# A two-layer hybrid backbone step in float32: 24 rows of the prompt tile's expert products moved out of the attention heads, scores taken negated, one inverse root for four gate inputs

## What is computed

```python
h = x * (1.0 + scale1) + shift1
q, k, v, su, sv = project_heads(h, w_in)        # su, sv through gelu
attn = latent_attention(q, k, v, ctx_k, ctx_v, sink)   # 8 heads; softmax over [sink, scores]
sg = u * (einsum('gpq,bnqgc->bnpgc', w_s, layer_norm(v)) + b_s)   # u = su, v = sv
y = concatenate([attn, sg]) @ w_o
x = layer_norm(ALPHA * x + gate1 * y)
h = x * (1.0 + scale2) + shift2
...
q = (x @ w_q).reshape(n, 8, 2, 128)             # peer(h, ...)
s1, s2 = q[:, :, 0] @ key1.T, q[:, :, 1] @ key2.T
idx, g = top 16 of the sums of the two top 16   # per token and head: 128 experts of 16384
a = einsum('thkd,td->thk', u_tab[idx], h)       # "u rows": dot products
out = einsum('thk,thkd->td', gelu(a) * g, v_tab[idx])  # "v rows": weighted sum
x = layer_norm(ALPHA * x + gate2 * out)
```

## Time and profile before

| | |
|---|---|
| median of 3 runs | 3826.93 us (3823.88 to 3830.95) |
| the profiled execution, its own time | 3821.99 us |
| its span, first to last instruction | 3820.2 us |
| PE busy | 3482.8 us (91%) |
| VectorE busy | 2808.7 us (74%) |
| ScalarE busy | 855.0 us (22%) |
| GpSimd busy | 1600.8 us (42%) |
| HBM traffic | 330 GB/s over the span |
| mean granted clock of PE | 0.946 |

### The profile page before, as it was taken

One profiled execution on the slowest core, in us unless ns is written; L12 is line 12 of the kernel. 1 busy time (PEld: TensorE's weight loads), 2 busy tenths in 40 slices (PEclk: granted clock), 3 DMA queues, 4 the chain that ended last, 5 costly groups with the idle time before them and its releaser, 6 DMA issues.

```text
span 3820.2 us, 38450 instructions
## 1 busy us (share of the span) xinstructions
PE 3482.8 (91%) x12478; PEld 2127.3 (56%) x12478; DVE 2808.7 (74%) x6205; ACT 855.0 (22%) x2198; POOL 1600.8 (42%) x1362
## 2 busy tenths in 40 slices
PE   6897889998889999999988878999988999999996
PEld 2554445888778444444336443478877864444443
DVE  1489769878776875666756897698877768766668
ACT  1104301156642000000021151111765210000000
POOL 2046336213641355555510761542146323555553
PEclk9896889999999999999989878999998999999998
DMA  9877569878999999999984974888899998999995
GB/s 345 326 264 281 187 231 346 315 262 304 409 399 327 352 355 414 413 413 413 386 311 137 368 247 139 295 329 317 282 345 408 377 357 314 388 413 414 413 404 230
DMA packets 413991, 1263.48 MB, mean 331 GB/s; under 512 B 36241, under 2 KB 139665, under 8 KB 370785
## 3 DMA queue, kind: packets, MB, share of 16 engines
q0 software_dynamic: 192000, 721.61, 49.3%
q1 hardware_dynamic: 171808, 514.19, 36.0%
q10 hardware_dynamic: 49984, 25.23, 2.2%
HBM read 1174.06 MB, written 86.84 MB: 330 GB/s over the span
## 4 chain that ended last, share of the span: by engine, by line
PE 48%; DMA 22%; DVE 16%; POOL 7%; issue 6%; ACT 1%; ACTq 0%; SPq 0%; DVEq 0%; POOLq 0%
PE P L919 23%; DMA ring<-in_peer_u_dram,eidx 10%; DMA ring<-in_peer_v_dram,eidx 10%; POOL ring L660 7%; PE P L893 6%; PE T L931 5%; DVE ring L1268 5%; PE P L947 4%; PE P L743 4%; DMA ring<-in_w_mod_dram 2%; PE V L947 1%; PE O L947 1%; DVE h L1286 1%; PE T L726 1%; PE T L905 1%
## 5 line engine op out<-in xcount | busy, mean ns | idle before, releaser
L660 POOL DMA_INDIRECT ring<-in_peer_u_dram,eidx x768 | 939.9, 1224 | 1300.9 <-DVE ring L1268 810.1
L1268 DVE SCALAR_TENSOR_TENSOR ring<-ring,h 128x1024 f32<-128x1024 f32 x768 | 925.0, 1223 | 278.5 <-DMA ring<-in_peer_u_dram,eidx 258.1
L947 PE MATMUL P<-w_ring,area 128*128 128x512 f32 x2048 | 933.9, 599 | 44.4 <-DVE area L1442 44.4
L919 PE MATMUL P<-hT,w_ring 128*128 128x256 f32 x4096 | 925.0, 384 | 0.0
L660 POOL DMA_INDIRECT ring<-in_peer_v_dram,eidx x512 | 621.1, 1213 | 673.9 <-DVE late L1286 401.4
L919 PEld LDWEIGHTS P<-hT,w_ring 128*128 128x128 f32 x4096 | 781.9, 194 | 103.9
L947 PEld LDWEIGHTS P<-w_ring,area 128*128 128x128 f32 x2048 | 390.7, 192 | 549.8 <-issue 549.6
L1286 DVE SCALAR_TENSOR_TENSOR h<-ring,dots,h 128x1024 f32<-128x1024 f32 x254 | 326.0, 1283 | 157.7 <-DMA ring<-in_peer_v_dram,eidx 144.5
L1286 DVE SCALAR_TENSOR_TENSOR late<-ring,dots,late 128x1024 f32<-128x1024 f32 x254 | 325.6, 1282 | 18.2 <-DMA ring<-in_peer_v_dram,eidx 2.8
L893 PE MATMUL P<-hT,w_ring 128*128 128x128 f32 (+1 forms) x1024 | 289.1, 444 | 2.9 <-issue 2.2
L947 PE MATMUL V<-w_ring,qT 128*128 128x512 f32 x512 | 261.4, 592 | 0.0
(11 more groups left out here) (219 smaller groups left out, 3367.2 us busy)
## 6 DMA issues: line engine op xcount, KB each, us to landing
w_ring<-in_peer_uT_dram SPq DMA_DIRECT2D x128, 1024.0 KB
w_ring<-in_peer_vB_dram SPq DMA_DIRECT2D x128, 1024.0 KB
ring<-in_w_mod_dram POOLq DMA_DIRECT2D x48, 1024.0 KB, 8.3
w_ring<-in_peer_wq_dram SPq DMA_DIRECT2D x64, 512.0 KB
h<-acts_d SPq DMA_DIRECT2D x64, 512.0 KB
w_ring<-in_w_in_dram SPq DMA_DIRECT2D x48, 512.0 KB
area<-gate_d SPq DMA_DIRECT2D x16, 1536.0 KB, 14.6
hT<-gate_d SPq DMA_DIRECT2D x16, 1536.0 KB, 12.9
```

The lines of the kernel that those rows point to most:

```text
L660: pool.indirect_dma_start(out=ring[:, b, :], out_offset=None, in_=tables["uv".index(phase)], in_offset=bass.IndirectOffsetOnAxis(ap=eidx[: ...
L919: mm = pe.matmul(out[:, 0:TOKENS], w[:, c * P:(c + 1) * P], hT[:, c, TOKENS:2 * TOKENS], start=c == 0, stop=c == DC - 1)
L947: mm = pe.matmul(bank[ACC[2 * t + half]][:, :], w, uv_ring[:, b // 2 % (WR // 2), b % 2, half * 512:(half + 1) * 512], start=b == 0, stop= ...
L1268: dve.scalar_tensor_tensor(ring[:, b, :], ring[:, b, :], 1.0, h2[:, k, :], ALU.mult, ALU.mult, accum_out=dots[:, k, row:row + 1]).then_inc ...
```

## The change

Five edits, in the order of the program:

1. *Rows.* `prompt_rows` now counts rows. In group S: 16 in the projection and 24 ahead of the attention as before; behind a head 1, in heads 2 and 5 of each tile 2 (40 in all, before 64); 8 behind the last head and the wait for `rows_in`, ahead of the first residual; 40 behind the residuals (before 24). ScalarE's `gelu_dots(0)` stands ahead of query block 4 instead of 2, and VectorE's `expert_weights(0)` and v rows begin at key block 4 instead of 3: the same 64 rows over 12 key blocks instead of 13.
2. *Negated scores.* VectorE scales by -1/8, adds the mask and takes the minimum with the negated sink; what it gets is the negated maximum. The instruction L1530 and its semaphore are gone; ScalarE's exponentials take `scale=-1.0` and wait for the score bank's emptied counter. The sinks are negated once per layer, in group P.
3. *One inverse root.* `sv_stats` takes the statistics of all the group's tiles ahead of the first head and computes their inverse roots together, in columns of the tensor `r1`. `norm_sv` keeps the scaling and the two products.
4. *Positions in the u sweep.* Slot transposes behind blocks 45, 77 and 104 (before 47, 78 and 105). Chunks from block 48 over 28 blocks, from 79 over 23, from 106 over 17 (before 50 over 27, 80 over 22, 107 over 16).
5. ScalarE's `top_softmax` and `gelu_dots(1)` stand one or two blocks earlier.

```diff
-SLOT_BLOCKS = {47: 3, 78: 4, 105: 1}
-CHUNK_BLOCKS = [(3, 50, 27), (4, 80, 22), (1, 107, 16)]
+SLOT_BLOCKS = {45: 3, 77: 4, 104: 1}
+CHUNK_BLOCKS = [(3, 48, 28), (4, 79, 23), (1, 106, 17)]
...
-                            act.wait_ge(probs_max, l * (TILES * HEADS) + (k * HEADS + h + 1))
-                            act.activation(esink[:, h:h + 1], sink[:, h:h + 1], ACT.Exp, bias=negmax[:, k % 2, h:h + 1]
-                                           ).then_inc(sink_exp, 1)
+                            job = ("score", g, t, h)
+                            act.wait_ge(emptied[BANK[job]], emptied_at(job, l))
+
+                            act.activation(esink[:, h:h + 1], sink[:, h:h + 1], ACT.Exp, scale=-1.0,
+                                           bias=negmax[:, k % 2, h:h + 1]).then_inc(sink_exp, 1)
...
-                        if g == "S" and j == 2:
+                        if g == "S" and j == 4:
                             gelu_dots(0)
...
+                def sv_stats(g):
+
+                    nt = len(GROUPS[g])
+                    for t in range(nt):
+                        job = ("in", g, 3, t)
+                        dve.wait_ge(emptied[BANK[job]], emptied_at(job, l))
+                        link(dve.bn_stats(stats[:, 0, :], sv[:, t, :]))
+                        link(dve.bn_aggr(sv_mean[:, t, :], stats[:, 0:1, :]))
+                    var, y, half, other = sv_mean[:, 0:nt, 1], sv_rstd[:, 0:nt], sv_nr[:, 0, 0:nt], sv_nr[:, 1, 0:nt]
+                    note(dve.tensor_scalar(half, var, EPS, -0.5, ALU.add, ALU.mult))
+                    link(dve.tensor_scalar(other, var, EPS, None, ALU.add))
+                    link(dve.tensor_single_scalar(other.bitcast(U32), other.bitcast(U32), 1, ALU.logical_shift_right))
+                    link(dve.tensor_scalar(y.bitcast(U32), other.bitcast(U32), -1.0, float(0x5f3759df), ALU.mult, ALU.add))
+                    for _ in range(3):
+                        link(dve.tensor_tensor(other, y, y, ALU.mult))
+                        link(dve.tensor_tensor(other, other, half, ALU.mult))
+                        link(dve.scalar_tensor_tensor(y, other, 1.5, y, ALU.add, ALU.mult))
+
                 def norm_sv(g, t):
-                    job = ("in", g, 3, t)
-                    dve.wait_ge(emptied[BANK[job]], emptied_at(job, l))
-                    layer_norm_stats(sv[:, t, :], AW)
+                    link(dve.tensor_scalar(sv[:, t, :], sv[:, t, :], sv_mean[:, t, 0:1], sv_rstd[:, t:t + 1],
+                                           ALU.subtract, ALU.mult))
...
+                    if g == "P":
+                        link(dve.tensor_scalar(sink[:], sink[:], -1.0, None, ALU.mult))
+                    sv_stats(g)
...
-                                                           HD ** -0.5, sink[:, h:h + 1], ALU.add, ALU.max,
-                                                           maxs[:, k % 2, h:h + 1]), job)
-                            dve.tensor_scalar(negmax[:, k % 2, h:h + 1], maxs[:, k % 2, h:h + 1], -1.0, None,
-                                              ALU.mult).then_inc(probs_max, 1)
+                                                           -HD ** -0.5, sink[:, h:h + 1], ALU.add, ALU.min,
+                                                           negmax[:, k % 2, h:h + 1]), job)
...
-                                prompt_rows(1)
+                                prompt_rows(2 if h in (2, 5) else 1)
...
                     dve.wait_ge(rows_in, (2 * l + (gi + 1)) * 48)
+                    if latent:
+
+                        prompt_rows(GP)
...
-                        prompt_rows(12)
+                        prompt_rows(SLOTS - 24 - 16 - 40 - GP)
...
-                        if latent and j == 3:
+                        if latent and j == 4:
                             expert_weights(0)
-                        if latent and j >= 3:
-                            add_rows(0, PV_EARLY * (j - 3) // 13, PV_EARLY * (j - 2) // 13)
+                        if latent and j >= 4:
+                            add_rows(0, PV_EARLY * (j - 4) // 12, PV_EARLY * (j - 3) // 12)
```

24 lines of the change are left out of this document (12 added, 12 removed).

## The result

The changed kernel takes 3802.31 us (median of 4 runs, 3794.20 to 3804.24), the kernel before 3828.94 beside it (4 runs, 3823.88 to 3833.62). The ratio is 0.9924, with a 95% interval of 0.9909 to 0.9939: 29 us less by the ratio, where 77 were forecast. The direction was right; 3802 lies outside the range of 3730 to 3786.

The account below looks back on a forecast made before the run. The prediction took VectorE to bound the latent attention, PE the u sweep, and left the v sweep unchanged. Per layer, -31 us in attention and -7.5 in query and u sweep gave 3827 - 77 = 3750 us, range 3730 to 3786.

Parts of the forecast that it names:

- The sum, -38.5 us per layer: Whole kernel: attention -31 and query and u sweep -7.5 us per layer, -77 us for both layers.
- Rows between the heads, -27.2 us per layer: Latent attention: 64 rows between heads become 40, so 24 x 1.135 = 27.2 us leave VectorE per layer.
- PE takes over the attention: Rival: PE's 100 us at clock 0.73 plus 17 us of waits limit the attention's gain to 15.5; 3781 us, chance 0.13.
- Negation and root, -8.1: Latent attention: removing the negation saves VectorE 2.6 us and the shared inverse root 5.5 us per layer.
- 8 rows ahead of the residuals: 0: After the last head: the rows may overrun VectorE's wait, but the last projection tile sets the end; cost 0, at most 3 us.
- 40 rows end at T+62, PE keeps 5.7 us: Behind the last residual tile, done at T: rows end at T+62, ahead of block 4's key products; PE stays 5.7 us earlier.
- VectorE 6 to 7 us later against T: After keys and their 64 rows, taking 109 us as before, VectorE is 6 to 7 us later against the last residual's end.
- PE waits about 5 us at the slots, -7.5 us for query and u sweep: Tile 3's slot transposes, u sweep: PE waits about 5 us for VectorE, yet the transposes come 7.5 us earlier per layer.
- From there on the one-hots set the pace: U sweep behind tile 3's slots: one-hots set the pace, and PE's wait of 8.42 us falls to about 5.
- The burst starves: Rival: the sixteen added gathers behind the residuals run slowly, rows end 12 us later; 3775 us, chance 0.18.
- Slower: Rival: PE's clock stays at 0.50 through the attention, so PE needs 147 us there; 3839 us, chance 0.03.
- Nothing: Rival: what leaves the heads comes back whole in the burst and the sweep; 3827 us, chance 0.02.

Follow-up runs that it names:

- e9: The change with tile 3's exponentials behind block 41, 24 rows between the heads instead of 40 and 56 behind the residuals instead of 40: 3809.3 us, one run.
- e4: The kernel before with only the negation gone from the heads and the one inverse root; rows and places as before: 3803.6 us, ratio 0.9933.
- e8: e1 with the 8 rows ahead of the residuals moved behind them, 48 there: 3807.9 us, ratio 0.9942.
- e1: The change with only tile 3's exponentials moved, from behind u block 33 to behind block 41: 3782.5 us, ratio 0.9875.
- e11: e6 with tile 4's slot transposes behind block 74 instead of 77, chunks of tiles 3 and 4 over 26 blocks each: 3771.3 us.
- e15: The kernel before with the change's moved rows and places alone, without the negation and norm edits: 3817.7 us, ratio 0.9971.
- e6: The change with 48 rows between the heads instead of 40, 32 behind the residuals instead of 40, tile 3's exponentials behind block 39: 3770.9 us, ratio 0.9844.
- e12: e6 with the third head's score products of the latent group repeated seven times in place, in PE's wait ahead of its first share: 3768.2 us.
- e10: e6 with 8 of the 24 rows ahead of the first head moved between the heads (16 ahead, 56 between): 3758.1 us, ratio 0.9808.
- e14: e1 with 32 rows between the heads instead of 40 and 48 behind the residuals instead of 40: 3793.8 us, one run.
- e7: e4 with tile 3's exponentials behind block 38, its slots behind 43, its chunks from block 46 over 30 blocks: 3795.7 us, ratio 0.9910.

## Why the prediction was wrong

- **The sum, -38.5 us per layer.** In the profiled executions the attention gave 20.2 and 20.9 us, and from the projection's first product to the v sweep the layers took 12.4 and 14.2 us more where 7.5 less had been forecast. Together that is 14.5 us less for both layers. The two executions lie 19.8 us apart, of which 3.3 are their starts and 2.6 the way from one layer's v sweep to the next one's first score; the medians lie 27 apart.
- **Rows between the heads, -27.2 us per layer.** Wrong as a term. VectorE's time fell by that, but the stage didn't: by the series above, 24 rows less save 13 to 15 us. I charged 4 us for PE, and VectorE's waits for PE's scores came to 12.5. PE's clock was to rise above 0.8 and was 0.76. The rival "PE takes over the attention" had part of the mechanism: in the change PE is busy 101.7 us of 125 and waits 23.9, where the rival had 100 and 17. But it isn't a floor, as the 114.6 us of e9 show. The rival's numbers also mix two bases: 118 us is a length of the whole stage, 25 less than 143, while its gain of 15.5 is counted from 133 us of heads. The measured gain lies between 15.5 and 31, the measured length above both texts' lengths, 118 and 112.
- **The lower bound of 20.** It held, but its working doesn't: a third of PE's 73 us, done at the half clock, takes 24 us more, not 11.
- **Negation and root, -8.1.** Nearly right: e4 shows 7.1 in layer 0 and 5.7 in layer 1, where VectorE does set the pace. The time fell by 25 us where 16 had been expected of it, more than these terms give twice; that isn't explained.
- **Attention -31.** Measured -20.2 and -20.9, at the lower bound of 20.
- **8 rows ahead of the residuals: 0.** Right, and for the reason given: they begin behind the wait of 13.55 us, the first residual comes 7 us later, and the last tile makes up for it. e8 shows what the place is worth: with these rows behind the residuals, the slots come 10.7 us later.
- **40 rows end at T+62, PE keeps 5.7 us.** Right: T+63.2; the u sweep starts at T+132.4 for T+138.3 before, 5.9 earlier. ScalarE's activation came at 548.20, PE's key products at 549.14 with 0.35 us idle ahead of them.
- **VectorE 6 to 7 us later against T.** This step was mis-sized: 16.3 us. I let the keys and the 64 v rows take "the 109 us they took". But more of the v rows now fall under PE's sweep and its weights: they end 54 us behind the sweep's start, before 33. In both kernels their gathers fall behind some 30 us after that start. Before, the rows were all but done by then; now they wait 8.3 us where they waited 1.2, with DMA at 419 GB/s and a share of 1.02 from 647 to 660. These 7.1, 1.2 us from the burst and 1.1 at tile 1's first rows, on top of the 6.5 forecast, make 16. That DMA's load is the reason for the late gathers is read from the order in time; no run tests it.
- **PE waits about 5 us at the slots, -7.5 us for query and u sweep.** This is the step that failed. I followed VectorE's lateness to the slot transposes alone. It has an earlier reader, `top_softmax(3)` in ScalarE's queue, with PE's bank emptying queued behind it. ScalarE's wait there was 2.86 us; VectorE's 16.3, PE's 5.9 and the two blocks (6.9) add to it, which gives 32.0, the number measured (32.02). PE stood 22 us of it, and instead of 7.5 us earlier the slots came 11.1 later against T. From T to the v sweep it is 12.4 us longer, so of the 23.5 us by which T was earlier in layer 0 (some 3 of them the start of the execution) 11 are left. The stall alone is worth 20 us of the whole time, by e1; the rest of the loss is VectorE's lateness, since in e1 the slots come at T+304, as before the change, and not 7.5 us earlier.
- **From there on the one-hots set the pace.** The stretch behind the slots did keep its length: no run got it under 417.7 us. That the one-hots set it isn't shown, and e11 speaks against them alone. Since the length stays, the sum should have been read off the moment of tile 3's slots alone.
- **Prompt group: 0.** Right. From the prompt group's first score to its last, 87.1 to 108.0 us before and 83.5 to 102.2 after; but e15, with the old code there, has 84.3 to 101.9.
- **The rivals.** "The burst starves" saw late gathers in the wrong place: the rows of the burst came as forecast, the v rows behind it were late. Its argument that DMA and POOL are near full there was too strong: from 508 to 546 us before the change DMA is at 0.82 and POOL busy 28 of 38 us. "Slower" needed the clock at 0.50 throughout. The Trainium skill, in TensorE: Matmul & The Clock Gate, Part 4 (PE-mode transpose), says that transposes don't count as activity in the way that products do and that the full clock doesn't engage for them; this attention, full of them, reached a clock of 1.00 in every run whose stretches I read, so the forecast that I drew from the rule doesn't hold here. Whether the transposes count after all or the products among them were enough, no run tells. "Nothing" had the right shape for the rows: what they left between the heads came back behind T.

## What to carry to other kernels

When an edit makes an engine late against the others, follow every reader of what it produces, in the order of each reader's queue, and look at what stands behind that reader in the same queue: here a wait of 2.86 us that cost nothing sat ahead of the instructions that empty PE's banks. Work taken out of a stage where a second engine is 70% busy saves its whole duration only until that engine has to be waited for (here the first 8 rows of 40), and then less than half of it (0.44 of 1.135 us). Find the one moment from which the rest follows unchanged (here tile 3's slots, 418 to 425 us ahead of the v sweep in layer 0 of every run), and judge each placement by it.

## What was not expected of the hardware

PE's clock stood at 0.50 from 296 to about 332 us in the changed kernel, and in e6, e9 and e12, although PE was busy with hardly a pause from 313 on, and in e12 also from 293 to 306; in e10, where PE's last wait of over 1 us ended at 305, it rose in the stretch from 323 to 328. Later in the same stage of the change it fell behind two waits of 1.5 and 2.0 us (from 350 to 356), in e6 behind one of 3.1 (at 357), and was back at 1.00 or near it within 10 us of dense work; in e9 it stayed at 1.00 over single waits of 1.00 and 1.43 us. Why it takes longer the first time is open: e12 filled most of the first wait, and nothing moved. The other thing is that the start of an execution varies: the first latent score came at 290.2 us in e14 and at 295.1 in e7, which are alike up to there, and that is more than several of the terms of the sum.
